# An expert loop in which down weights are split like gate-up weights, one block runs ahead of another, and GpSimd forms the row mask

## What is computed

```python
def _moe(u, router_w, router_b, exp_w_gu, exp_w_down, shared_w_gu, shared_w_down):
    scores = jax.nn.sigmoid((u @ router_w).astype(jnp.float32))
    _, idx = lax.top_k(scores + router_b.astype(jnp.float32), TOP_K)
    ...
    routed = lax.map(lambda a: _routed_experts(a[0], a[1], a[2], exp_w_gu, exp_w_down), (u, idx, wts))
    return routed + _swiglu(u, shared_w_gu, shared_w_down)

def _swiglu(x, w_gu, w_down):          # w_gu: 1024 x 512, w_down: 256 x 1024 for each expert
    g, up = jnp.split(x @ w_gu, 2, axis=-1)
    return (jax.nn.silu(g) * up) @ w_down
```

## Time and profile before

| | us |
|---|---|
| median of 3 runs (lowest, highest) | 1602.52 (1600.34, 1602.64) |
| span of the profiled execution | 1598.8 |
| of it, first silu to last silu of the expert loop | 742.3 to 1555.5 |
| PE busy | 1357.2 (85%) |
| DVE busy | 939.1 (59%) |
| ACT busy | 635.9 (40%) |
| GpSimd busy | 247.8 (15%) |

### The profile page before, as it was taken

How to read it: one execution, slowest core, us unless ns; L and a number is a source line. 1 busy time by engine, 2 the same in 40 slices (tenths; PEclk the granted TensorE clock), 3 DMA queues, 4 the chain that set the end, 5 groups by cost and what they waited for, 6 DMA issues and landing times.

```text
span 1598.8 us, 26750 instructions
## 1 busy us (share of the span) xinstructions
PE 1357.2 (85%) x5742; PEld 975.4 (61%) x5743; DVE 939.1 (59%) x1838; ACT 635.9 (40%) x878; POOL 247.8 (15%) x311
## 2 busy tenths in 40 slices
PE   1699996779999978866989999898899998898990
PEld 0288874568888757534656666666566666565660
DVE  4713338968225876535776576776757556455544
ACT  1363225333213312224555354564555454334432
POOL 0000000000000000002222322323223223232320
PEclk9999998889999989887999999999999999999995
DMA  9412201133225856136999888998989888778743
GB/s 304 133 53 87 72 0 53 53 118 117 94 93 189 284 161 210 66 145 222 329 308 270 243 266 244 329 330 255 315 268 320 243 268 237 213 224 228 218 89 118
DMA packets 111191, 310.59 MB, mean 194 GB/s; under 512 B 16217, under 2 KB 19489, under 8 KB 110898
## 3 DMA queue, kind: packets, MB, share of 16 engines
q1 hardware_dynamic: 82176, 241.20, 43.8%
q0 software_dynamic: 20592, 54.03, 16.1%
q10 hardware_dynamic: 8386, 14.89, 2.6%
HBM read 305.34 MB, written 43.52 MB: 218 GB/s over the span
## 4 chain that ended last, share of the span: by engine, by line
PE 42%; DMA 22%; DVE 14%; issue 8%; ACT 6%; ACTq 4%; DVEq 2%; POOLq 1%; POOL 1%; SPq 0%
PE psum L1300 23%; DMA expert_sum<-y_rows,add_idx 12%; PE psum L1467 6%; PE psum L1484 4%; DMA xg<-u_rows,row_idx 4%; DMA gu_raw<-in_exp_w_gu 4%; PE psum L1275 4%; ACT gu_hi L800 2%; DVE tmp_tok L964 2%; ACT y_rows L823 1%; DVE gu_lo L1215 1%; PE psum L1367 1%; PE psum L1358 1%; POOL step_word L547 1%; PE psum L1474 1%
## 5 line engine op out<-in xcount | busy, mean ns | idle before, releaser
L1215 DVE TENSOR_TENSOR gu_lo<-gu_raw,gu_hi 128x1024 f32 x212 | 246.8, 1221 | 112.6 <-ACT gu_hi L800 112.4
L1484 PE MATMUL psum<-w_dn,mask 128*128 x560 | 260.4, 608 | 36.9 <-DVE mask L1235 36.9
L800 ACT ACTIVATE gu_hi<-gu_raw 128x1024 f32 x212 | 209.8, 1048 | 112.7 <-issue 76.4
L1467 PE MATMUL psum<-gu_hi,xT_hi 128*128 x560 | 240.6, 430 | 8.8 <-DVE xT_lo L1205 5.0
L1467 PE MATMUL psum<-gu_hi,xT_lo 128*128 x560 | 219.7, 392 | 0.0
L1467 PE MATMUL psum<-gu_lo,xT_hi 128*128 x560 | 219.1, 391 | 0.0
L1484 PEld LDWEIGHTS psum<-w_dn,mask 128*128 128x128 f32 x560 | 101.2, 190 | 144.6 <-issue 144.6
L400 DVE TENSOR_TENSOR w_lo<-ring,w_hi 128x1024 fp32r<-128x1024 f32 x80 | 95.2, 1223 | 94.5 <-ACT w_hi L393 92.4
L1300 PE MATMUL psum<-uT_hi,w_hi 128*128 128x512 f32 x352 | 138.7, 394 | 13.3 <-DVE w_lo L400 12.2
L823 ACT ACTIVATE y_rows<-psum,row_w 128x512 f32<-128x512 f32 x140 | 88.5, 682 | 147.2 <-DMA expert_sum<-y_rows,add_idx 140.9
L1467 PEld LDWEIGHTS psum<-gu_hi,xT_hi 128*128 128x128 f32 x560 | 105.7, 189 | 56.0 <-issue 36.2
(11 more groups left out here) (257 smaller groups left out, 1875.6 us busy)
## 6 DMA issues: line engine op xcount, KB each, us to landing
gu_raw<-in_exp_w_gu SPq DMA_DIRECT2D x212, 512.0 KB, 6.2
w_dn<-in_exp_w_down SPq DMA_DIRECT2D x70, 1024.0 KB
ring<-in_w_in SPq DMA_DIRECT2D x56, 512.0 KB, 5.2
ring<-in_ada_w SPq DMA_DIRECT2D x48, 512.0 KB, 4.6
ring<-in_w_branch_b SPq DMA_DIRECT2D x8, 512.0 KB, 5.1
ring<-in_w_branch_a SPq DMA_DIRECT2D x8, 512.0 KB, 5.4
ring<-in_w_out SPq DMA_DIRECT2D x8, 512.0 KB, 5.4
mods<-in_x ACTq DMA_DIRECT2D x1, 2048.0 KB, 13.0
```

What stands on the lines that cost most here:

```text
L800: act.activation(gu_hi[:, bass.ds(order % 2, 1), PK * p:PK * p + PK].rearrange("p o k f -> p (o k) f"), gu_raw[:, PK * p:PK * p + PK], ACT ...
L1215: tt(gu_lo[at].rearrange("p o k f -> p (o k) f"), gu_raw[:, PK * p:PK * p + PK], gu_hi[at].rearrange("p o k f -> p (o k) f").bitcast(F32), ...
L1467: mm = pe.matmul(moe_bank(GU), rows[:, k], w[:, gu_place, k].rearrange("p o n -> p (o n)"), start=(k == 0 and n == 0), stop=(k == KT - 1 a ...
L1484: mm = pe.matmul(moe_bank(Y0 + g), hT[:, j], w_dn[:, place, j, g * NC:(g + 1) * NC].rearrange("p o n -> p (o n)"), start=(j == 0), stop=(j ...
```

## The change

All of it lies in the expert loop and what leads into it. The down weights are loaded into the same raw buffer as the gate-up weights (`ew_raw`, three pieces of 1 MB: gate-up halves 0 and 1, down weights 2) and split into hi and lo as well; ACT copies h as `hT_hi` and DVE subtracts to `hT_lo`, and the down product becomes 12 matmuls of the fast format. `xT_hi`, `xT_lo` and `y_rows` have two places, `xg` two instead of three. ACT and DVE take 128x2048 in one instruction for weights, and 128x1024 for rows. On PE the gate-up product of block b+1 stands ahead of the down product of block b, and rows are found one block further ahead (`AHEAD`). `pick_rows` moves from DVE to GpSimd. Each expert's split stands in three places of a block's code, each with reads of its own from the tables. GpSimd clears two regions of `sum_dram`'s spare rows, one after the other, ahead of the loop. Some buffers used only ahead of or behind the loop lie elsewhere.

The diff, cut: of the functions that stand in full above only the new lines are shown.

```diff
-UNROLL, SPAN = 3, 6
+UNROLL, SPAN = 4, 4
 SPANS = -(-MOE_BLOCKS // (UNROLL * SPAN))
-TABLE = SPANS * SPAN * UNROLL + UNROLL
+AHEAD = 3
+TABLE = SPANS * SPAN * UNROLL + 2 * UNROLL
+HALVES = 3
...
-        gu_lo = sb("gu_lo", [P, 2, KT, 2 * DE], F32R, moe)
-        gu_raw = sb("gu_raw", [P, KT, 2 * DE], F32, moe)
-        w_dn = sb("w_dn", [P, UNROLL, 2, D], F32, moe)
+        sb("under_ew_hi", [P, 2, 2 * HALVES, D], F32, moe)
+        ew_lo = sb("ew_lo", [P, 2, 2 * HALVES, D], F32R, moe)
+        ew_raw = sb("ew_raw", [P, 2 * HALVES, D], F32, moe)
...
+        xT_hi = sb("xT_hi", [P, 2, KT, P], F32R, moe)
+        xT_lo = sb("xT_lo", [P, 2, KT, P], F32R, moe)
+        xg = sb("xg", [P, 2, D], F32, moe)
...
+        expert_gu = exp_w_gu[0].rearrange("e (p k) f -> e p (k f)", k=KT)
+        expert_dn = exp_w_down[0].rearrange("e (p j) n -> e p (j n)", j=2)
+        def ew_source(e, p):
+            one = expert_gu[bass.ds(e, 1), :, 2 * D * p:2 * D * p + 2 * D] if p < 2 else expert_dn[bass.ds(e, 1)]
+            return one.rearrange("o p n -> p (o n)")
+        def ew_place_of(w, order, p):
+            return w[:, bass.ds(order % 2, 1), 2 * p:2 * p + 2].rearrange("p o c n -> p (o c n)")
+        def ew_raw_of(p):
+            return ew_raw[:, 2 * p:2 * p + 2].rearrange("p c n -> p (c n)")
+        def gu_of(w, order, k):
+            return w[:, bass.ds(order % 2, 1), k // 2, k % 2 * NC:k % 2 * NC + NC].rearrange("p o n -> p (o n)")
+        def dn_of(w, order, j, g):
+            return w[:, bass.ds(order % 2, 1), 4 + j, g * NC:g * NC + NC].rearrange("p o n -> p (o n)")
...
+            for i, s, b in live_blocks(sp, ask=False):
                 fresh = sp.value_load(fresh_of[0:1, bass.ds(b, 1)], min_val=0, max_val=1)
                 with sp.If(fresh > 0):
                     e = sp.value_load(expert_of[0:1, bass.ds(b, 1)], min_val=0, max_val=E - 1)
                     order = sp.value_load(order_of[0:1, bass.ds(b, 1)], min_val=0, max_val=E)
+                    for p in range(HALVES):
+                        sp.wait_ge(ew_split, order * HALVES + p + 1)
+                        sp.dma_start(ew_raw_of(p), ew_source(e, p)).then_inc(ew_in[p], 16)
...
+            for s in range(2):
+                pool.dma_start(sum_dram[T:T + P], xg[:, 0]).then_inc(scattered, 16)
+                pool.wait_ge(scattered, 16 * s + 16)
...
+            def gather(n, s, at):
+                pool.wait_ge(idx_ready, n + 1)
+                step(at)
+                pool.indirect_dma_start(xg[:, s % 2], None, u2_dram, bass.IndirectOffsetOnAxis(row_idx[:, s], 0),
+                                        bounds_check=T - 1, oob_is_err=False).then_inc(gathered[s % 2], 16)
+            def pick_rows(n):
+                e = pool.value_load(expert_of[0:1, bass.ds(n, 1)], min_val=0, max_val=E - 1)
+                if not isinstance(n, int) or n:
+                    pool.wait_ge(idx_psum, n)
+                pool.tensor_tensor(rel[:], slot[:, :, bass.ds(e, 1)], block_start[:, bass.ds(n, 1)].unsqueeze(1).broadcast_to([P, TT, 1]), ALU.subtract).then_inc(rel_ready, 1)
+                pool.tensor_copy(pick_cols[:, :, 2:5], w3[:, :, bass.ds(e, 1), :].rearrange("p t o w -> p t (o w)")).then_inc(pick_ready, 1)
+                pool.wait_ge(rel_ready, n + 1)
+                pool.tensor_tensor(pick_word[:], ones[0:1, 0:1], ones[0:1, 0:1], ALU.mult)
+                for t in range(TT):
+                    own_loop = pool.tensor_scalar(pick[:, t], iota_row[:], rel[:, t], None, ALU.is_equal)
+                    own_loop.then_inc(pick_ready, 1)
+            pick_rows(0)
+            pick_rows(1)
             gather(0, 0, 0)
+            pick_rows(2)
             gather(1, 1, 1)
+            pick_rows(AHEAD)
+            pool.wait_ge(xT_psum, 1)
+            gather(2, 2, 2)
             for i, s, b in live_blocks(pool):
+                pool.wait_ge(xT_psum, b + 2)
+                gather(b + AHEAD, (s + AHEAD) % UNROLL, 2 * b + 3)
+                pick_rows(b + AHEAD + 1)
+                pool.wait_ge(scattered, 16 * b + 32)
+                pool.wait_ge(y_ready, b + 2)
                 pool.wait_ge(add_ready, b + 1)
+                step(2 * b + 4)
+                pool.indirect_dma_start(sum_dram, bass.IndirectOffsetOnAxis(add_idx[:, s % 2], 0), y_rows[:, s % 2], None,
                                         compute_op=ALU.add, bounds_check=T + P - 1, oob_is_err=True).then_inc(scattered, 16)
             live_n = pool.value_load(live_count[0:1, 0:1], min_val=1, max_val=MOE_BLOCKS)
+            pool.wait_ge(scattered, 16 * live_n + 32)
+            pool.wait_ge(step_done, 2 * live_n + 3)
+            pool.wait_ge(xT_ready, live_n + 2)
             pool.tensor_tensor(step_word[:], ones[0:1, 0:1], ones[0:1, 0:1], ALU.mult).then_inc(experts_done, 1)
...
+            def rows_hi(n, s):
+                act.wait_ge(xT_psum, n + 1)
+                act.activation(xT_hi[:, s % 2].rearrange("p k n -> p (k n)"), psum[:, 0:2, :].rearrange("p g n -> p (g n)"), ACT.Copy).then_inc(xT_hi_ready, 1)
+            def expert_hi(n, pieces):
                 fresh = act.value_load(fresh_of[0:1, bass.ds(n, 1)], min_val=0, max_val=1)
                 with act.If(fresh > 0):
                     order = act.value_load(order_of[0:1, bass.ds(n, 1)], min_val=0, max_val=E)
+                    for p in pieces:
+                        act.wait_ge(ew_in[p], order * 16 + 16)
+                        act.activation(ew_place_of(ew_hi, order, p), ew_raw_of(p), ACT.Copy).then_inc(ew_hi_ready, 1)
+            def silu(n):
+                act.wait_ge(gu_done, n + 1)
+                if not isinstance(n, int) or n:
+                    act.wait_ge(h_ready, n)
+                act.activation(gate_h, moe_bank(GU)[:, 0:DE], ACT.Silu).then_inc(silu_done, 1)
             act.wait_ge(tables_ready, 1)
             act.wait_ge(sum_started, 16)
+            act.nop().then_inc(y_ready, 1)
+            expert_hi(0, (0, 1))
+            rows_hi(0, 0)
+            rows_hi(1, 1)
+            expert_hi(0, (2,))
+            expert_hi(1, (0,))
+            silu(0)
+            expert_hi(1, (1,))
             for i, s, b in live_blocks(act):
+                act.wait_ge(hT_psum, b + 1)
+                act.activation(hT_hi[:].rearrange("p j n -> p (j n)"), moe_bank(HT)[:, 0:2 * P], ACT.Copy).then_inc(hT_hi_ready, 1)
+                rows_hi(b + 2, s)
+                expert_hi(b + 1, (2,))
+                expert_hi(b + 2, (0,))
+                silu(b + 1)
+                expert_hi(b + 2, (1,))
                 act.wait_ge(idx_ready, b + 1)
                 act.wait_ge(scattered, 16 * b + 16)
+                act.wait_ge(y_psum, b + 1)
+                act.activation(y_rows[:, s % 2], psum[:, Y0:Y0 + 2, :].rearrange("p g n -> p (g n)"), ACT.Copy, scale=row_w[:, s:s + 1]).then_inc(y_ready, 1)
...
+            def expert_lo(n, pieces):
                 fresh = dve.value_load(fresh_of[0:1, bass.ds(n, 1)], min_val=0, max_val=1)
                 with dve.If(fresh > 0):
                     order = dve.value_load(order_of[0:1, bass.ds(n, 1)], min_val=0, max_val=E)
+                    for p in pieces:
+                        dve.wait_ge(ew_hi_ready, order * HALVES + p + 1)
+                        tt(ew_place_of(ew_lo, order, p), ew_raw_of(p), ew_place_of(ew_hi, order, p).bitcast(F32), ALU.subtract).then_inc(ew_split, 1)
+            def gated_up(n):
+                dve.wait_ge(silu_done, n + 1)
+                if not isinstance(n, int) or n:
+                    dve.wait_ge(hT_psum, n)
+                tt(h_tok, gate_h, moe_bank(GU)[:, DE:2 * DE], ALU.mult).then_inc(h_ready, 1)
+            dve.nop().then_inc(ew_split, HALVES)
+            for n in range(AHEAD):
                 find_rows(n, n)
+            expert_lo(0, (0, 1))
+            rows_lo(0, 0)
+            rows_lo(1, 1)
+            expert_lo(0, (2,))
+            expert_lo(1, (0,))
+            gated_up(0)
+            expert_lo(1, (1,))
             for i, s, b in live_blocks(dve):
+                dve.wait_ge(hT_hi_ready, b + 1)
+                tt(hT_lo[:].rearrange("p j n -> p (j n)"), moe_bank(HT)[:, 0:2 * P], hT_hi[:].rearrange("p j n -> p (j n)").bitcast(F32), ALU.subtract).then_inc(hT_ready, 1)
+                dve.wait_ge(y_ready, b + 1)
+                find_rows(b + AHEAD, (s + AHEAD) % UNROLL)
+                dve.wait_ge(scattered, 16 * b + 16)
+                dve.tensor_copy(add_idx[:, s % 2], row_idx[:, s]).then_inc(add_ready, 1)
...
+            def turn_rows(n, s, uses):
+                pe.wait_ge(gathered[s % 2], uses)
+                if not isinstance(n, int) or n:
+                    pe.wait_ge(xT_ready, n)
+                for k in range(KT):
+                    mm = pe.transpose(moe_bank(k // 4)[:, (k % 4) * P:(k % 4 + 1) * P], xg[:, s % 2, bass.ds(k, P, KT)], ident[:])
+                mm.then_inc(xT_psum, 1)
+            def gate_up(n, s, order):
+                pe.wait_ge(xT_ready, n + 1)
```

(23 more changed lines are left out.)

189 lines of the change are left out of this document (38 added, 151 removed).

## The result

The changed kernel takes 1686.19 us (median of 4 runs, 1677.66 to 1688.85) against 1602.3 for the kernel before (median of 4 runs): ratio 1.0511, 95% interval 1.0481 to 1.0541. I had forecast 1598.5, in a range of 1574 to 1638. The profiled execution has a span of 1675.9 us, 77.1 more than before. It splits at two silus: that of block 1 comes at 764.65 instead of 753.65 (+11.0), the loop to block 69's takes 853.5 instead of 801.8 (+51.7), and from there to the end it is 57.8 instead of 43.3 (+14.4).

A forecast was written before the change was run, and what follows sets the result against it. PE's own order was taken to set the period. Loop -18.4, way in +7.0 and way out +7.4 gave -4.0 us: span 1594.8, plus 3.7 between span and median, 1598.5 us; range 1574 to 1638.

The forecast's parts named there:

- Loop: Silu of block 1 to silu of block 69: 39 x 12.1 + 12 x 11.8 + 17 x 10.0 = 783.5 us, 18.4 less.
- Way in: Ahead of block 1's silu: second clearing, masks formed on GpSimd, then the closed chain; +7.0 us.
- Way out: Behind the last silu: two down products, transposes, a gate-up of a nonexistent block, an evacuation; 13.9 us, +7.4.
- the port: Rival, chance 0.20: GpSimd masks over 0.42 us wait for DVE's third subtraction, delaying gate-up; +31 to +47, 1630 to 1645 us.
- late loads: Rival, chance 0.20: 1 MB weight pieces land in 7.8 to 8.3 us, dense blocks take 12.6; +20, 1618 us.
- Blocks without new weights, 10.0 us: Blocks needing no new expert weights: from 11.71 us to 10.0, bounds 9.8 and 10.8, by a shorter down product and fewer waits.
- The closed chain, 11.7 us: Fresh blocks: gate-up, silu, table reads, ACT's copy, DVE's subtraction, next gate-up sum to 11.7 us; PE waits 1.8.
- Dense blocks, 12.1 us: Fresh blocks in dense stretches: chain of 11.7 plus 0.4 us for late loads and masks; bounds 11.7 and 12.8.
- the saving of the down product: Twelve fast matmuls take 0.8 us less per block; in fresh blocks this was to count for nothing.
- Gathers: Rows found a block earlier: mean gather wait of 0.28 us goes; GpSimd's scatter-to-gather path takes 20.2 us for two blocks.

The follow-up runs named there:

- The pair with gathers four ahead: Changed kernel with rows gathered four blocks ahead instead of three: 1663.75 us; the same with two float32 matmuls filling PE's pause: 1618.84 us.
- the reads ahead: Changed kernel with ACT's two table reads for block b+2 made once, ahead of silu, and used for both copies: 1680.80 us, ratio 1.0505.
- half the bytes: Changed kernel with table reads ahead, gathers four ahead and one filling matmul, loading only half of each weight piece (output differs): 1589.49 us, one run.
- four filling matmuls: Changed kernel with four float32 matmuls that feed nothing, ahead of gate-up where the next block is fresh: 1696.70 us, ratio 1.0591.
- the two slow runs with masks on DVE in groups of six: Changed kernel, table reads ahead, masks on DVE: find four ahead, gathers three, 1694.16 us; gathers four ahead, find behind gate-up, masks behind last subtraction, 1698.49 us.

## Why the prediction was wrong

The miss in the profiled execution is 1675.9 - 1594.8 = 81.1 us. Loop: 853.5 against 783.5 forecast, 70.0. Way in: +11.0 against +7.0, 4.0. Way out: +14.4 against +7.4, 7.0. The 0.38 that I gave to a slower kernel lay on two rivals, the port and late loads, and neither made this result.

- **Blocks without new weights, 10.0 us:** right in kind. Twelve of the 17 take 9.54 to 9.87 us, and the down product takes 2.7 us, as worked out. But late gathers make five longer, up to 14.7, and the mean is 10.49: 8 us of the 70.
- **The closed chain, 11.7 us, with a wait of 1.8:** right in kind. 13 fresh intervals at full clock average 11.9 us, and the usual pause is 2.1.
- **Dense blocks, 12.1 us: the step that failed.** I gave 0.4 us to late loads and masks and took gate-up at 5.6 us as it was before, when PE hardly stopped. But the pause that I had forecast is itself what lowers the clock, and gate-up is a link of the chain, so its slow matmuls lengthen the round: 33 intervals of 13.50 us, 33 x (13.50 - 12.1) = 46 of the 70 us. Five more of 14.8 to 15.3 us, with the clock fallen as well, waited about 3 us for masks (four) or rows (one): 14 us. That the saving of the down product "only lengthens that wait" was wrong, as a wait had a price through the clock that I had put at nothing. The pair with gathers four ahead shows it: 39 us of loop for a filled pause. The Trainium skill (TensorE: Matmul & The Clock Gate, HAM oscillation) describes waits for loads that bring every tile back to 1.2 GHz, and advises to order the loop so that such waits don't stand between its tiles; I had not weighed it. The trace agrees in kind, with the granted clock at 0.87, though the waits of the page's example are longer than the 2.1 us here.
- **The port (rival, 0.20):** its mechanism was seen, its price was not. A mask takes 0.60 us undisturbed where I had taken 0.3, so the condition of the rival (over 0.42) was met. Yet in the changed kernel PE waits 20.4 us for masks in all, and 54.9 once the chain is 10.7 us. The slow clock seems to give the masks time: the four waits of 2.7 to 3.5 us all follow a block at full clock. The Trainium skill (GPSIMD Engine Reference, Engine selection) has one-input work near line rate; the row has 0.60 against 0.35 on DVE, and the measurement decides.
- **Loads late (rival, 0.20):** not in the changed kernel, where 1 MB of gate-up weights lands in 5.7 us in the median and ACT's copies wait 5.6 us for loads in all. With the reads ahead (chain 10.7 us) it lands in 7.7, and half the bytes took 23 us off the loop.
- **Gathers:** I had them 20.2 us per two blocks and the mean wait gone. 17.3 us stayed, and they took over in nearly all the runs that touched only the clock, the masks or the chain (35.6 to 53.6 us; 23.3 with four filling matmuls, where PE itself was full).
- **Way in:** 4.0 more. The silu of block 0 comes at 751.3 instead of 748.7; the masks of the first two blocks, both formed ahead of the first gather, take 2.35 us each instead of 1.2. The first interval then takes 13.4 us instead of 11.7, at a clock of 0.74.
- **Way out:** from silu to the end of the last `y_rows` 13.4 us (forecast 13.9). Missed: GpSimd then walks through the tables of the dead blocks, 15.24 us instead of 7.73. Behind the 70 live blocks `UNROLL, SPAN = 4, 4` leaves ten dead ones in the span that has begun, 3, 6 only two; the dead spans, of which one word each is read, are five in both. With 6, 3 (two and five again) it is 8.2.

What stays open: how much each limit costs by itself in the changed kernel, since they cover each other; and how much of the two slow runs with masks on DVE in groups of six is DVE's standstill (64.0 and 57.6 us of idle time) and how much the placing of find and masks.

## What to carry to other kernels

When a change lets the busiest engine wait in every round, ask what the wait does to its clock before counting it as free; if the work that then runs slowly is itself a link of the chain that makes the engine wait, every round gets longer by it. In a loop with several limits close together, one repair shows nothing (seven runs between 1677 and 1697 us), and the right pair shows all: read which wait takes over and remove both. And on an engine that issues transfers in order, look for what stands ahead of the urgent one: the gather was late behind a scatter, whatever was found earlier. When a loop's body grows, look at the queue of the kind "instruction" before blaming the new order.

## What the runs showed of the hardware

- Two float32 matmuls (1.7 us) in a pause of 2.1 us kept the granted clock at 1.00 in all 68 intervals, where 41 had fallen without them.
- In the changed kernel the clock held at 1.00 in 11 of the 16 fresh intervals that follow a block without new weights, but in only 2 of the 34 that follow another fresh block.
- Four 128x128 masks on GpSimd: 2.35 us alone, 6.09 beside two 128x2048 subtractions.
- A GpSimd loop over empty blocks is not free: 15.24 us of table reads for ten dead blocks and five dead spans, 7.73 for two and five, so 0.94 us for a block.
- With masks on DVE and six blocks in a group, DVE stood still for up to 7.4 us at the start of a group, while q14 ("instruction") moved 69 packets in the loop; with groups of four, or without the masks, it moved 3 and 5.
